# One level of Strassen-Winograd multiplication for a float32 input projection, in three token passes

## The chip, the cores and the metric

The kernel runs on one core of one Trainium2 chip. The metric is the device time of one execution in microseconds (us), taken as the median of several runs. All stages (short convolution, its output projection, keys and values, stick-breaking attention, decoding) are in one program, and each stage starts behind a barrier of all engines.

## What is computed

The change touches the first layer, a gated short convolution over 2048 prompt frames and 8 x 16 = 128 sample frames (2176 tokens, D = 1024):

```python
def _short_conv_mixer(xn, prev, w_in, conv_w, w_out):
    proj = xn @ w_in
    b_gate, c_gate, h, z = jnp.split(proj, 4, axis=-1)
    u = c_gate * h
    T = u.shape[1]
    up = jnp.concatenate([prev.astype(u.dtype), u], axis=1)
    conv = conv_w[0] * up[:, 0:T]
    for i in range(1, CONV_WIDTH):
        conv = conv + conv_w[i] * up[:, i:i + T]
    y = jax.nn.silu(z) * b_gate * conv
    return y @ w_out, up[:, T:]
```

Here `xn` is the RMS-normed input, `w_in` is 1024 x 4096, and the convolution is 3 taps wide. A layer adds the normed result to x.

## The kernel before

A float32 product is made of three fp32r products: every operand is split into a high part (a rounded copy) and a low part (the rest), and `project` (L349) issues high x high, high x low and low x high for each 128 rows of the contraction, eight times over K = 1024.

**Norming.** `phase_norm_in` (L112) takes the 17 tiles of 128 tokens. Per tile SP loads 512 KB; ACT squares and sums it and takes the root (L185, L188); DVE inverts (L209) and scales (L212); PE transposes it with 8 products by the identity (L248); ACT copies the result out of PSUM as the high part `a_xh` (L195) and DVE subtracts for the low part `a_xl` (L221). From the fifth tile on PE puts parts of the first strip's projection between the transposes (`project_group`, L231), so that it works while later tiles are normed. POOL splits the weights: two multiplications by the norm's gain and a subtraction of 128x1024 elements per strip (L285, L287, L289 in `split_weights`).

**Projection.** `phase_conv` (L408) then goes over 8 channel blocks c, and for each over the four matrices in the order c gate, h, z, b. Such a pair is called a strip here: 1024 x 128 weights against all 2176 tokens, in five groups of 512, 512, 384, 384, 384 tokens (`GROUPS`, L27), each in a PSUM bank of its own: 5 x 24 = 120 matmuls, 32 strips. PE waits at L487 for the group's bank to be read out, and at L485 for the split weights, of which there are two sets (names w_ and c_). ACT reads the c gate (L502) and z through SiLU (L506); DVE makes u = c * h (L537), the taps (L551 to L561), and the two gates (L566, L571); SP stores y for each block (L443). POOL runs one strip ahead (`weight_stream`, L308).

**Border to the output projection.** `Border` (L365) holds what the next stage, `phase_out` (L611), needs first: the first y tile, and the 8 row blocks of `a_w_out`, of which four are copied high (L399) and two low (L404) before the barrier. PE's first matmul of `phase_out` is at L762.

Of the kernel before, what the change touches and what calls it, by code (L numbers as in the profile page):

```python
# [111 lines left out]
def phase_norm_in(nc, x_prompt, x_sample, ident, ident_r, ident_in, epsb, xh, xl, consts, order, gain_in, room, pg):  # L112

    with ExitStack() as ctx:
        sb, pb, sem, sem2 = make_tools(nc, ctx)
        S = 4
        x_in = sb("n_x", [P, S, D])
        xs_at = (nc.sbuf_base + 31) // 32 * 32  # L120
        xs = sb("n_xs", [P, S, D])
        xs_bits = nc.alloc_sbuf_tensor_at("n_xs_bits", [P, S, D], F32R, offset=xs_at)
        junk = sb("n_junk", [P, D])
        ss = sb("n_ss", [P, S])
        std = sb("n_std", [P, S])
        rstd = sb("n_rstd", [P, S])
        ps = pb("n_ps", [P, 2, KT // 2, P])
        x_loaded = sem2("n_x_loaded", S)
        squared, std_ready, rstd_ready = sem2("n_squared", S), sem2("n_std", S), sem2("n_rstd", S)
        xs_ready, turned, hi_done, lo_done = sem2("n_xs_ready", S), sem2("n_turned"), sem2("n_hi"), sem2("n_lo")  # L130
        eps_set, ident_loaded, consts_loaded = sem("n_eps_set"), sem("n_ident_loaded"), sem("n_consts_loaded")
        ident_set = sem("n_ident_set")
        raw_loaded, gain_loaded, next_loaded = sem2("n_raw_loaded"), sem("n_gain_loaded"), sem("n_next_loaded")
        hi_ready, scaled, split = sem("n_w_hi"), sem("n_w_scaled"), sem("n_w_split")
        projected, passed, warm = sem("n_projected"), sem("n_passed"), sem("n_warm")
        HK = KT // 2
        raw, _, _, (gain, _) = room
        block = ctx.enter_context(nc.Block())

        @block.sync  # L140
        def _(sp):
            def load(j, s):
                sp.wait_ge(xs_ready[s], j)
                if is_sample(j, s, S):
                    src = x_sample
                else:
                    src = x_prompt[bass.ds((S * j + s) * P, P), :]
                sp.dma_start(x_in[:, s, :], src).then_inc(x_loaded[s], 16)

            for t in range(S):  # L150
                load(0, t)
                if t == 0:
                    sp.dma_start(ident[:, :], ident_in).then_inc(ident_loaded, 16)
            for m in range(2):
                sp.dma_start(raw[:, m, :, :], order[m][0](0)).then_inc(raw_loaded[m], 16)
            with sp.Fori(1, NT // S) as j:
                for s in range(S):
                    load(j, s)
            load(NT // S, 0)
            for dst, src in consts:  # L160
                sp.dma_start(dst, src, allow_slow_non_contiguous=True).then_inc(consts_loaded, 16)
            sp.wait_ge(consts_loaded, 16 * len(consts))

        @block.gpsimd
        def _(pool):
            load_gains(pool, [gain], [gain_in], gain_loaded)
            pool.wait_ge(gain_loaded, 16)
            for s in range(2):
                pool.wait_ge(raw_loaded[s], 16)
                split_weights(pool, room, s, order[s][1], hi_ready, scaled, split, s)  # L170
                pool.wait_ge(split, s + 1)
                apart(pool, passed)
                pool.dma_start(raw[:, s, :, :], order[2 + s][0](0)).then_inc(next_loaded, 16)
            pool.wait_ge(next_loaded, 32)

        @block.scalar
        def _(act):
            act.wait_ge(eps_set, 1)
            act.activation(std[:, 0:1], epsb[:, :], ACT.Sqrt).then_inc(warm, 1)
            act.wait_ge(warm, 1)  # L180

            def sums(j, s):
                act.wait_ge(x_loaded[s], 16 * (j + 1))
                act.wait_ge(rstd_ready[s], j)
                act.activation(junk[:, :], x_in[:, s, :], ACT.Square,  # L185
                               accum_out=ss[:, s:s + 1]).then_inc(squared[s], 1)
                act.wait_ge(squared[s], j + 1)
                act.activation(std[:, s:s + 1], ss[:, s:s + 1], ACT.Sqrt, scale=1.0 / D,  # L188
                               bias=epsb[:, :]).then_inc(std_ready[s], 1)

            def high(j, s):
                t = S * j + s
                for h in range(2):
                    act.wait_ge(turned[h], t + 1 + S * h)
                    act.activation(xh[:, h * HK:(h + 1) * HK, bass.ds(t * P, P)], ps[:, h, :, :],  # L195
                                   ACT.Copy).then_inc(hi_done[h], 1)

            token_tiles(act, sums, high, slots=S)
            act.activation(std[:, S - 1:S], epsb[:, :], ACT.Silu).then_inc(warm, 1)

        @block.vector
        def _(dve):
            dve.memset(epsb[:, :], EPS).then_inc(eps_set, 1)
            dve.wait_ge(ident_loaded, 16)
            dve.tensor_copy(ident_r[:, :], ident[:, :]).then_inc(ident_set, 1)

            def scale(j, s):
                dve.wait_ge(std_ready[s], j + 1)
                dve.reciprocal(rstd[:, s:s + 1], std[:, s:s + 1]).then_inc(rstd_ready[s], 1)  # L209
                dve.wait_ge(rstd_ready[s], j + 1)  # L210
                dve.wait_ge(turned[1], S * j + s + 1)
                dve.tensor_scalar(xs[:, s, :], x_in[:, s, :], rstd[:, s:s + 1], None,  # L212
                                  ALU.mult).then_inc(xs_ready[s], 1)

            def low(j, s):
                t = S * j + s
                at = bass.ds(t * P, P)
                for h in range(2):
                    half = slice(h * HK, (h + 1) * HK)
                    dve.wait_ge(hi_done[h], t + 1)  # L220
                    dve.tensor_tensor(xl[:, half, at], ps[:, h, :, :], xh[:, half, at].bitcast(F32),  # L221
                                      ALU.subtract).then_inc(lo_done[h], 1)

            token_tiles(dve, scale, low, slots=S)

        @block.tensor
        def _(pe):
            pe.sem_inc(turned[1], S)
            pe.wait_ge(ident_set, 1)

            def project_group(g, kt0, kt1):  # L231
                a, n = GROUPS[g]
                if kt0 == 0:
                    pe.wait_ge(split, 1)
                    for h in range(2):
                        pe.wait_ge(lo_done[h], (a + n) // P)
                mm = project(pe, pg[g][:, 0:n], room[1][0], room[2][0], xh, xl, a, n, kt0, kt1)
                if kt1 == KT:
                    mm.then_inc(projected, 1)

            for t in range(NT):
                j, s = divmod(t, S)
                pe.wait_ge(xs_ready[s], j + 1)
                for h in range(2):
                    wait_past(pe, lo_done[h], t)
                    for i in range(HK):
                        kt = h * HK + i
                        mm = pe.transpose(ps[:, h, i, :].bitcast(F32R), xs_bits[:, s, kt * P:(kt + 1) * P],  # L248
                                          ident_r[:, :])
                    mm.then_inc(turned[h], 1)  # L250
                for g in range(NG - 1):
                    t0, n = GROUPS[g + 1][0] // P, GROUPS[g + 1][1] // P
                    if t0 <= t < t0 + n:
                        project_group(g, (t - t0) * KT // n, (t - t0 + 1) * KT // n)
            project_group(NG - 1, 0, KT)
            pe.wait_ge(projected, NG)
# [12 lines left out]
def whole_room(sb, tag, room):  # L269

    raw, wh, wl, gains = room
    return raw, wh + [sb(tag + "wh1", [P, KT, P], F32R)], wl + [sb(tag + "wl1", [P, KT, P], F32R)], gains
# [2420 lines left out]
```

## Time and profile before

| | before |
|---|---|
| median of 3 runs | 2816.25 us (2815.89 to 2818.65) |
| the profiled execution | 2820.25 us, of which the span from first to last instruction 2818.7 us |
| granted TensorE clock, mean | 0.993 |
| PE busy | 2755.2 us (98%) |
| DVE, ACT, POOL busy | 1645.2, 1315.5, 1156.5 us |
| DMA | 433.33 MB, 154 GB/s on average |

The page cuts the span into 40 slices of 70 us; the convolution lies in the first 11 of them. PE reads 9 (90% or more) in each but the first, while DVE, ACT and POOL read 0 to 4 in most of them after the first two. A busy PE is not a PE at its peak: what a matmul costs is read from the distance between the starts of neighbours in the timeline, since its own duration includes its way through the array.

### The profile page before, as it was taken

The page shows a single profiled execution, that of the slowest core. Times are in us where ns is not written, and L with a number is a line of the kernel's source. Part 1 is how long each engine was busy: PE and PEld are TensorE (multiplying, and loading weights), DVE is VectorE, ACT ScalarE, POOL GpSimd, SP SyncE. Part 2 cuts the span into 40 slices and gives each one's busy share as a digit, 9 for nine tenths or more (in the row PEclk, how much of TensorE's full clock was granted, in tenths as well). Part 3 has the DMA queues.
Part 4 walks back from the last instruction along what each step waited for, and adds up shares of the span by engine and source line. Part 5 has one row for each costly group of instructions (what it writes and reads, how often), then busy time and mean ns, then how long its engine had stood idle before and what let it go on. Part 6 is the DMA issues. An engine that isn't in the chain of part 4 may idle for free. (4 is left out here: it accounts for less than half of the span.)

```text
span 2818.7 us, 42045 instructions
## 1 busy us (share of the span) xinstructions
PE 2755.2 (98%) x14856; PEld 2409.4 (85%) x14856; DVE 1645.2 (58%) x2152; ACT 1315.5 (47%) x2733; POOL 1156.5 (41%) x1023
## 2 busy tenths in 40 slices
PE   7999999999999999999989999999999999979998
PEld 6999999999978888889978888888888888868886
DVE  5321232123244450102249999999999999998775
ACT  6000000000034441111148888888888888875543
POOL 3333333233210020002356877777777768651110
PEclk9999999999999999999999999999999999999999
DMA  5101110111064444424578676777777866766873
GB/s 160 38 24 38 38 38 22 38 38 38 9 202 131 136 152 153 174 102 157 166 219 269 197 245 198 237 215 217 223 222 207 251 203 207 224 184 203 239 229 107
DMA packets 280359, 433.33 MB, mean 154 GB/s; under 512 B 52578, under 2 KB 218594, under 8 KB 274180
## 3 DMA queue, kind: packets, MB, share of 16 engines
q1 hardware_dynamic: 269156, 391.41, 45.4%
q0 software_dynamic: 11040, 39.86, 4.7%
q8 instruction: 89, 1.46, 0.2%
q14 instruction: 74, 0.61, 0.1%
HBM read 307.40 MB, written 123.81 MB: 153 GB/s over the span
## 5 line engine op out<-in xcount | busy, mean ns | idle before, releaser
L1994 POOL TENSOR_TENSOR a_a<-a_a,a_prod 128x512 f32<-128x512 f32 (+3 forms) x640 | 661.1, 1051 | 270.3 <-DVE a_prod L1945 196.0
L1945 DVE TENSOR_TENSOR_SCAN a_prod<-a_keep,a_prod,a_restart 128x513 f32<-128x513 f32 x384 | 478.0, 1269 | 7.5 <-ACT a_keep L1889 5.7
L1888 ACT ACTIVATE a_a<-a_pz 128x512 f32<-128x512 f32 (+3 forms) x640 | 357.4, 559 | 69.4 <-PE a_pz L1815 44.4
L1955 DVE TENSOR_TENSOR a_atl<-a_pt,a_ath 128x512 fp32r<-128x512 f32 (+3 forms) x640 | 363.0, 599 | 33.0 <-ACT a_ath L1898 29.9
L1889 ACT ACTIVATE a_keep<-a_pz 128x512 f32<-128x512 f32 (+3 forms) x640 | 361.4, 565 | 0.0
L1898 ACT ACTIVATE a_ath<-a_pt 128x512 fp32r<-128x512 f32 (+3 forms) x640 | 333.0, 558 | 57.8 <-PE a_po L1829 34.2
L1838 PEld LDWEIGHTS a_pt<-ident_r,a_bits 128*128 128x128 f32 x2176 | 231.4, 141 | 51.1 <-DVE a_atl L1955 7.4
L285 POOL TENSOR_TENSOR w_wh<-w_raw,w_gain 128x1024 fp32r<-128x1024 f32 x22 | 41.7, 1897 | 534.2 <-PE v_pg L355 278.9
L1814 PE MATMUL a_pz<-a_kh,a_q 128*128 128x512 f32 (+3 forms) x640 | 246.9, 389 | 8.7 <-ACT a_keep L1889 6.2
L1827 PE MATMUL a_po<-a_ath,a_v 128*128 128x512 f32 (+3 forms) x640 | 250.8, 396 | 2.7 <-POOL a_v L2005 1.9
L1838 PE MATMUL a_pt<-ident_r,a_bits 128*128 128x128 f32 x2176 | 244.2, 241 | 6.4 <-DVE a_atl L1955 4.2
L1815 PE MATMUL a_pz<-a_kl,a_q 128*128 128x512 f32 (+3 forms) x640 | 233.7, 367 | 0.0
L353 PE MATMUL c_pg<-a_xh,w_wh 128*128 128x384 f32 (+1 forms) x640 | 231.3, 361 | 0.0
L353 PE MATMUL c_pg<-a_xh,c_wh 128*128 128x384 f32 (+1 forms) x640 | 230.7, 360 | 0.3 <-ACT c_cgate L502 0.3
L354 PE MATMUL c_pg<-a_xl,w_wh 128*128 128x384 f32 (+1 forms) x640 | 230.5, 360 | 0.0
L354 PE MATMUL c_pg<-a_xl,c_wh 128*128 128x384 f32 (+1 forms) x640 | 230.5, 360 | 0.0
L355 PE MATMUL c_pg<-a_xh,c_wl 128*128 128x384 f32 (+1 forms) x640 | 230.4, 360 | 0.0
L1829 PE MATMUL a_po<-a_atl,a_v 128*128 128x512 f32 (+3 forms) x640 | 229.7, 368 | 0.0
L355 PE MATMUL c_pg<-a_xh,w_wl 128*128 128x384 f32 (+1 forms) x640 | 228.9, 358 | 0.0
L537 DVE TENSOR_TENSOR c_u<-c_pg,c_cgate 128x512 f32<-128x512 f32 (+2 forms) x40 | 23.4, 585 | 317.9 <-PE c_pg L355 317.9
L1939 DVE TENSOR_TENSOR_SCAN a_prod<-a_keep,a_restart 128x128 f32<-128x128 f32 (+3 forms) x256 | 197.1, 805 | 9.0 <-ACT a_keep L1889 8.2
L506 ACT ACTIVATE c_sz<-c_pg 128x384 f32<-128x384 f32 (+1 forms) x40 | 21.4, 536 | 355.8 <-PE c_pg L355 355.8
(234 smaller groups left out, 6128.0 us busy)
## 6 DMA issues: line engine op xcount, KB each, us to landing
a_x<-x_d SPq DMA_DIRECT2D x84, 896.0 KB, 6.7
a_x<-x_d SPq DMA_DIRECT2D x56, 832.0 KB, 5.9
a_kh<-kh_t SPq DMA_DIRECT2D x32, 512.0 KB, 6.9
a_kl<-kl_t SPq DMA_DIRECT2D x32, 512.0 KB, 8.8
w_raw<-in_a_w_in POOLq DMA_DIRECT2D x30, 512.0 KB, 4.8
x<-f_xn POOLq DMA_DIRECT2D x17, 512.0 KB, 5.9
g_y_in<-sz_t SPq DMA_DIRECT2D x17, 512.0 KB, 7.9
g_x<-x SPq DMA_DIRECT2D x17, 512.0 KB, 3.6
```

The costliest lines, as they stand in the source:

```text
L353: pe.matmul(out, w_h[:, kt, :], x_h[:, kt, r], start=(kt == 0), stop=False)
L354: pe.matmul(out, w_h[:, kt, :], x_l[:, kt, r], start=False, stop=False)
L355: mm = pe.matmul(out, w_l[:, kt, :], x_h[:, kt, r], start=False, stop=(kt == KT - 1))
L1814: pe.matmul(o, lhs, kh2[hh][:, p0:p0 + w], start=True, stop=False)
L1827: pe.matmul(o, v2[hh][:, kb, :, :], ath[:, b % AS, c0:], start=first, stop=False, skip_group_check=True)
L1838: mm = pe.transpose(pt[:, turn_slot(pr, hh, b), q * P:(q + 1) * P].bitcast(F32R), a_bits[:, unit_slot(hh, u), q, j * P:(j + 1) * P], ident ...
L1888: act.activation(a[:, s, q, 0:w], pz[:, n % ZS, 0:w], ACT.Sigmoid, scale=SCALE)
L1889: act.activation(keep[:, n % KS, 0:w], pz[:, n % ZS, 0:w], ACT.Sigmoid, scale=-SCALE).then_inc(z_used, 1)
L1898: act.activation(ath[:, b % AS, c0:], pt[:, turn_slot(pr, hh, b), c0:], ACT.Copy).then_inc(at_hi, 1)
L1945: dve.tensor_tensor_scan(prod[:, s, 0:w + 1][:, ::-1], keep[:, n % KS, 0:w + 1][:, ::-1], restart[:, 0:1].broadcast_to([P, w + 1]), prod[: ...
L1955: dve.tensor_tensor(atl[:, b % AS, c0:], pt[:, turn_slot(pr, hh, b), c0:], ath[:, b % AS, c0:].bitcast(F32), ALU.subtract).then_inc(at_spl ...
L1994: pool.tensor_tensor(part, part, prod[:, n % PS, after:after + w], ALU.mult).then_inc(weighted, 1)
```

## The change

The projection's operands are cut in two along both dimensions: K into two halves of 512, a pair of weight matrices (c gate and h, or z and b) as the two output halves, and the tokens of a pass into two halves. The four output quarters then come from seven products instead of eight, by Winograd's form: the weights enter as A11, A12, A22 and four sums S1 to S4, the tokens as B11, B21, B22 and four differences T1 to T4. The outputs are put together by five additions out of PSUM.

- The tokens go in three passes, of 2 x 320, 2 x 384 and 2 x 384. A pass has 16 strips (8 channel blocks x 2 pairs of matrices), a strip 7 products, a product 4 x 3 = 12 matmuls of 320 or 384 columns: 84 a strip, 4032 in all (before: 3840 of 512 or 384).
- The weights are loaded anew in each pass, 1 MB a strip, now by SP's queue. POOL makes S1 to S4 (`sums`, four operations of 128x512). ACT makes every high part (seven of 128x512 a strip), DVE every low part. The gain is multiplied into the tokens (`stage`), no longer into the weights.
- Only the first 5 tiles are normed ahead; the other 12 are normed in odd strips of passes 0 and 1, all of the scaling by ACT.
- At the first strip of a pass each of the seven token operands (512 rows x 320 or 384 tokens, 4 x w elements a partition) is split anew by ACT and DVE, just before its product needs it, and POOL makes the differences (DVE two of them in pass 0).
- u = c * h, the gates and the last product move from DVE to POOL, out of SBUF; the first tap moves to ACT.
- SP's queue now carries the weight loads, the x tiles and the y stores in one written order.
- In `Border` five blocks of `a_w_out` are split high and low before the barrier.

PE's order in a strip n is A11, S1, A22 of strip n - 1, S2, A12, S4, S3. Its core, and what each product waits for:

```diff
+PASSES = [(0, 320), (640, 384), (1408, 384)]
...
+                if n >= 2 and i == A11_B11:
+                    pe.wait_ge(c11_read, n - 1)
...
+                elif i == A12_B21:
+                    pe.wait_ge(p1_read, n + 1)
+                elif i == S4_B22:
+                    pe.wait_ge(v_read, n + 1)
+                elif i == S3_T3:
+                    pe.wait_ge(u2_read, n + 1)
+                elif i == A22_T4:
+                    pe.wait_ge(c22_read, n + 1)
+                if first_of_pass(n):
+                    pe.wait_ge(x_lo[i], p + 1)
+                pe.wait_ge(w_lo[i], n + 1)
+                o = bank(n, b, w)
+                for k in range(NH):
+                    x_h, x_l = room.xh[i][:, k, 0:w], room.xl[i][:, k, 0:w]
+                    pe.matmul(o, room.wh[i][:, k, :], x_h, start=fresh and k == 0, stop=False, skip_group_check=True)
+                    pe.matmul(o, room.wh[i][:, k, :], x_l, start=False, stop=False, skip_group_check=True)
+                    mm = pe.matmul(o, room.wl[i][:, k, :], x_h, start=False, stop=k == NH - 1, skip_group_check=True)
...
+            for t in range(FIRST_TILES):
+                turn(t)
+            for n in range(NSTRIP):
...
+                product(n, A11_B11)
+                product(n, S1_T1)
+                if n:
+                    product(n - 1, A22_T4)
+                product(n, S2_T2)
+                product(n, A12_B21)
+                product(n, S4_B22)
+                product(n, S3_T3)
```

DVE's strip, and SP's and POOL's:

```diff
+                if n:
+                    c22(n - 1)
+                    low(n, S3_T3)
+                low(n + 1, A11_B11)
+                dve.wait_ge(done[S1_T1], n + 1)
...
+                add(room.v[:, 0:w], n, BANK_B, room.p1[:, n % 2, 0:w], v_read)
+                low(n + 1, S1_T1)
+                if n:
+                    c21(n - 1)
+                low(n, A22_T4)
...
+                add(room.u2[:, 0:w], n, BANK_C, room.p1[:, n % 2, 0:w], u2_read)
+                low(n + 1, S2_T2)
+                if n % 2:
+                    taps(n)
+                low(n + 1, A12_B21)
...
+                if n >= 0 and n + 2 < NSTRIP:
+                    sp.wait_ge(w_lo[A22_T4], n + 1)
+                    sp.wait_ge(summed, 4 * (n + 1))
+                    apart(sp, passed_sp)
+                    load_raw(n + 2, 1)
+                if n >= 2 and n % 2 == 0:
+                    store(n - 1)
...
+                if n and n % 2:
+                    set_u(n - 1, 1)
+                if n + 1 < NSTRIP:
+                    sums(n + 1)
+                if n and n % 2 == 0:
+                    gate(n - 1, 0)
+                    gate(n - 1, 1)
+                    finish(n - 1, 1)
```

How the instructions stand. First DVE in one channel block of the projection before (u, the edge copies, the taps; `c_t` is the convolved tile):

```order
L537 TENSOR_TENSOR c_u<-c_pg,c_cgate 128x512 x2
L537 TENSOR_TENSOR c_u<-c_pg,c_cgate 128x384 x2
L537 TENSOR_TENSOR c_u<-c_pg,c_cgate 128x256
L539 TENSOR_TENSOR c_us<-c_pg,c_cgate 128x8x16
L547 COPY c_edge<-c_u 128x2
L548 COPY c_edge<-c_us 128x16
L551 TENSOR_SCALAR c_t<-c_u,c_cw 128x2048
```

And DVE now in strip 15, the last of pass 0, from the middle of which the operands of pass 1 are split (`c_wl` and `c_xl` are low parts of weights and tokens, `c_pc` is PSUM, `c_v`, `c_sums`, `c_u_118` take its sums):

```order
L699 TENSOR_TENSOR c_wl_84<-c_raw_91,c_wh_77 128x512
L692 TENSOR_TENSOR c_xl_70<-c_stage,c_xh_63 128x1536
L706 TENSOR_TENSOR c_v<-c_pc,c_p_117 128x320
L699 TENSOR_TENSOR c_wl_85<-c_s_107,c_wh_78 128x512
L692 TENSOR_TENSOR c_xl_71<-c_t_94,c_xh_64 128x1536
L706 TENSOR_TENSOR c_sums<-c_pc,c_p_117 128x320
L699 TENSOR_TENSOR c_wl_90<-c_raw_92,c_wh_83 128x512
L706 TENSOR_TENSOR c_u_118<-c_pc,c_p_117 128x320
L699 TENSOR_TENSOR c_wl_86<-c_s_108,c_wh_79 128x512
L692 TENSOR_TENSOR c_xl_72<-c_stage,c_xh_65 128x1536
L727 SCALAR_TENSOR_TENSOR c_t<-c_u,c_taps,c_t 128x640 x2
```

Before, DVE touched PSUM or the convolution's tiles only; now the reads of PSUM that PE waits for stand in one queue with the splits of weights and tokens.

POOL before, one pair of strips (`w_raw` is the loaded weight tile):

```order
L285 TENSOR_TENSOR w_wh<-w_raw,w_gain 128x1024
L287 TENSOR_TENSOR w_raw<-w_raw,w_gain 128x1024
L289 TENSOR_TENSOR w_wl<-w_raw,w_wh 128x1024
L326 DMA w_raw<-in_a_w_in 128x8x128
L285 TENSOR_TENSOR c_wh<-w_raw,w_gain 128x1024
```

And POOL now at the same strip 15 (`c_s` are the weight sums, `c_stage` and `c_t_94` hold the tokens and T1):

```order
L865 TENSOR_TENSOR c_u<-c_sums,c_cg 128x320
L817 TENSOR_TENSOR c_s_107<-c_raw_91 128x512
L820 TENSOR_TENSOR c_s_108<-c_s_107,c_raw_91 128x512
L822 TENSOR_TENSOR c_s_109<-c_raw_91 128x512
L825 TENSOR_TENSOR c_s_110<-c_raw_91,c_s_108 128x512
L839 TENSOR_TENSOR c_stage<-c_stage,c_t_94 128x4x384
L865 TENSOR_TENSOR c_u<-c_sums,c_cg 128x320
L845 TENSOR_TENSOR c_stage<-c_stage 128x4x384
```

The weight DMAs are gone from POOL's queue; in it are now the sums, the products of the gating, and between them at a pass's end the token differences.

## Rows read from the trace of the kernel before

**Rows 1.** Windows: us, then each engine's busy time, PE clock, DMA share
```profile
22.20:61.20 39.00, 36.93 (x218) 31.04 (x218) 27.79 (x49) 29.77 (x61) 7.06 (x4) 1.00 0.50 148
62.13:794.70 732.57, 732.57 (x3728) 667.31 (x3728) 191.26 (x212) 48.03 (x86) 221.02 (x118) 1.00 0.12 38
```

**Rows 2.** Waits from 62 to 797 us: total, times, longest
```profile
DVE c_u L537 <- PE c_pg L355: 317.9, 40, 27.0
...
POOL c_wh L285 <- PE c_pg L355: 237.8, 15, 17.4
...
PE c_pg L353 <- ACT c_cgate L502: 0.3, 1, 0.3
```

**Rows 3.** Groups by shape, two of PE's twelve for the projection
```profile
L354 PE MATMUL c_pg<-a_xl,w_wh 128*128 128x384 f32 x384 | 129.0, 336 | 0.0
...
L353 PE MATMUL c_pg<-a_xh,c_wh 128*128 128x512 f32 x256 | 101.6, 397 | 0.3 <-ACT c_cgate L502 0.3
```

**Rows 4.** Timeline of PE: start, duration; 24 matmuls apart, then 20 apart
```profile
786.65 0.34 PE L355 MATMUL c_pg<-a_xh,c_wl 128*128 128x384 f32 x1
...
790.81 0.34 PE L355 MATMUL c_pg<-a_xh,c_wl 128*128 128x384 f32 x1
...
2697.28 0.29 PE L2323 MATMUL s_pzo<-s_kth,s_pad_h 128*128 128x272 f32 x1
...
2699.79 0.29 PE L2325 MATMUL s_pzo<-s_kth,s_pad_l 128*128 128x272 f32 x1
```

**Rows 5.** Timeline of the start and of the norming
```profile
4.64 1.06 ACT L185 ACTIVATE n_junk<-n_x 128x1024 f32<-128x1024 f32 x1 [2.15 <-issue]
...
8.48 1.06 ACT L185 ACTIVATE n_junk<-n_x 128x1024 f32<-128x1024 f32 x1 [2.37 <-DMA n_x<-in_x_prompt]
...
22.23 0.76 PE L353 MATMUL c_pg<-a_xh,w_wh 128*128 128x512 f32 x1
...
38.06 0.80 PE L248 MATMUL n_ps<-ident_r,n_xs_bits 128*128 128x128 f32 x8
38.70 0.47 PE L353 MATMUL c_pg<-a_xh,w_wh 128*128 128x512 f32 x1
```

**Rows 6.** Timeline of PE across the barrier before the output projection
```profile
794.45 0.34 PE L355 MATMUL c_pg<-a_xh,c_wl 128*128 128x384 f32 x1
797.31 0.47 PE L762 MATMUL f_ph<-b_xh,f_yh 128*128 128x512 f32 x1 [2.52 <-PEq L102]
...
798.68 0.63 PE L764 MATMUL f_ph<-b_xh,f_yl 128*128 128x512 f32 x1
799.11 0.63 PE L762 MATMUL f_ph<-b_xh,f_yh 128*128 128x512 f32 x1
```

**Rows 7.** Timeline of POOL, then of DVE, where both work from SBUF
```profile
280.03 2.41 POOL L289 TENSOR_TENSOR c_wl<-w_raw,c_wh 128x1024 fp32r<-128x1024 f32 x1
...
278.12 1.92 DVE L552 TENSOR_SCALAR c_t<-c_us,c_cw 128x128 f32<-128x128 f32 x1
280.07 4.52 DVE L554 SCALAR_TENSOR_TENSOR c_t<-c_u,c_cw,c_t 128x2048 f32<-128x2048 f32 x1
...
284.88 2.35 DVE L559 SCALAR_TENSOR_TENSOR c_t<-c_u,c_cw,c_t 128x2048 f32<-128x2048 f32 x1
```

**Rows 8.** Groups and timeline rows that price the new operations
```profile
L2018 POOL TENSOR_TENSOR w_raw<-w_raw,w_gain 128x512 f32<-128x512 f32 x26 | 27.1, 1042 | 23.6 <-POOLq L102 21.6 <-PE a_pq L1858 1.9
...
797.16 6.91 DVE L404 TENSOR_TENSOR b_xh<-b_x,b_xh 128x1024 fp32r<-128x1024 f32 x6 [1.77 <-PEq L102]
...
L571 DVE TENSOR_TENSOR c_sz<-c_pg,c_t 128x384 f32<-128x384 f32 x24 | 13.4, 558 | 79.0 <-PE c_pg L355 79.0
...
797.14 3.90 ACT L399 ACTIVATE b_xh<-b_x 128x1024 fp32r<-128x1024 f32 x4 [4.07 <-PEq L102]
...
L502 ACT ACTIVATE c_cgate<-c_pg 128x384 f32<-128x384 f32 x24 | 11.6, 494 | 76.3 <-PE c_pg L355 76.3
...
w_raw<-in_a_w_in POOLq DMA_DIRECT2D x30, 512.0 KB, 4.8
```

More of the change, by code:

```diff
@@ L109, in make_tools @@
     return sb, pb, sem, sem2
[L112 to L256, printed above, removed]
@@ L405, in low_weights @@
                               self.wh(kt, slice(0, D)).bitcast(F32), ALU.subtract).then_inc(self.w_lo, 1)
[L408 removed]
+NH = KT // 2
+PASSES = [(0, 320), (640, 384), (1408, 384)]
+PW_MAX = 384
+NPASS = len(PASSES)
+STRIPS = [(p, c, m) for p in range(NPASS) for c in range(KT) for m in range(2)]
+NSTRIP, PER_PASS = len(STRIPS), 2 * KT
+FIRST_TILES = 2 * PASSES[0][1] // P
+A11_B11, S1_T1, S2_T2, A12_B21, S4_B22, S3_T3, A22_T4 = range(7)
@@ new lines, in _ @@
+            sp.wait_ge(y_stored[0], 16 * KT)
+            for i in (A11_B11, A12_B21, A22_T4):
+                sp.wait_ge(w_lo[i], LAST)
+            sp.wait_ge(summed, 4 * LAST)
+            apart(sp, passed_sp)
+            border.load_tile(sp)
+            for i in (A11_B11, S1_T1):
+                sp.wait_ge(done[i], NSTRIP)
+            apart(sp, passed_sp)
+            border.load_weights(sp, range(AHEAD, KT))
+            sp.wait_ge(e_rows, 2)
+            apart(sp, passed_sp)
+            sp.dma_start(conv_p, room.edge_rows[0:2, :]).then_inc(e_stored, 16)
@@ new lines, in turn @@
+            def turn(t):
+                pe.wait_ge(scaled, t + 1)
+                out = turned_at(t)
+                wait_past(pe, staged, 2 * (t - 1 if t < FIRST_TILES else t))
+                if t == FIRST_TILES:
+                    pe.wait_ge(st_ready, 1)
+                for kt in range(KT):
+                    mm = pe.transpose(out[:, kt, :].bitcast(F32R), room.norm_bits[room.scaled(t)][:, kt * P:(kt + 1) * P],
+                                      ident_r[:, :])
+                mm.then_inc(turned, 1)
@@ new lines, in _ @@
+            act.wait_ge(eps_set, 1)
+            act.activation(room.std[:, 0:1], epsb[:, :], ACT.Sqrt).then_inc(warm, 1)
+            act.wait_ge(warm, 1)
+            for t in range(FIRST_TILES):
+                sums_of(t)
+                if t:
+                    scale(t - 1)
+                if t == 3:
+                    high_w(0, A11_B11)
+                elif t == 4:
+                    high_x(0, A11_B11)
+            scale(FIRST_TILES - 1)
+            high_w(0, S1_T1)
+            high_x(0, S1_T1)
@@ L576, in begin_next, with inverse, stage @@
-            def begin_next(g):
-                if g == 1:
+            def inverse(t):
+                dve.wait_ge(std_ready, t + 1)
+                dve.reciprocal(room.rstd[:, t:t + 1], room.std[:, t:t + 1]).then_inc(rstd_ready, 1)
+            def stage(t):
+                p = next(p for p in range(NPASS) if t * P < sum(tokens_of(p)[::2]))
+                at = t * P - PASSES[p][0]
+                dve.wait_ge(turned, t + 1)
+                if t == 0:
+                    dve.wait_ge(gain_loaded, 16)
+                for h in range(2):
+                    half = slice(NH * h, NH * (h + 1))
+                    dve.tensor_tensor(room.stage[:, half, at:at + P], turned_at(t)[:, half, :],
+                                      gain[:, half].unsqueeze(2).broadcast_to([P, NH, P]), ALU.mult).then_inc(staged, 1)
@@ new lines, in add, with c22, c21 @@
+            def add(out, n, b, other, read):
+                w = width(n)
+                dve.tensor_tensor(out, bank(n, b, w), other, ALU.add).then_inc(read, 1)
+            def c22(n):
+                w = width(n)
+                dve.wait_ge(done[S3_T3], n + 1)
+                wait_past(dve, u_set if n % 2 else y_done, 2 * pair(n) + (1 if n % 2 else -1))
+                dve.wait_ge(v_read, n + 1)
+                add(room.sums[:, 1, 0:w], n, BANK_C, room.v[:, 0:w], c22_read)
+            def c21(n):
+                w = width(n)
+                dve.wait_ge(done[A22_T4], n + 1)
+                wait_past(dve, u_set if n % 2 else y_done, 2 * (pair(n) + n % 2))
+                add(room.sums[:, 0, 0:w], n, BANK_C, room.p1[:, n % 2, 0:w], c21_read)
@@ new lines, in _ @@
+            dve.memset(epsb[:, :], EPS).then_inc(eps_set, 1)
+            dve.wait_ge(ident_loaded, 16)
+            dve.tensor_copy(ident_r[:, :], ident[:, :]).then_inc(ident_set, 1)
+            dve.memset(room.u[:, 0:2], 0.0).then_inc(cleared, 1)
+            inverse(0)
+            for t in range(FIRST_TILES):
+                if t + 1 < FIRST_TILES:
+                    inverse(t + 1)
+                if t == 3:
+                    low(0, A11_B11)
+                stage(t)
+            dve.wait_ge(staged, 2 * FIRST_TILES)
@@ L580, in begin_next @@
                                       ALU.subtract).then_inc(border.y_lo, 1)
-                elif 2 <= g < 2 + LOW_AHEAD:
-                    border.low_weights(dve, range(g - 2, g - 1))
-            with dve.Fori(0, KT - 1) as c:
-                conv_and_gate(c)
-            conv_and_gate(KT - 1)
+                k = n - PER_PASS * (NPASS - 1) - 7
+                if 0 <= k < AHEAD:
+                    border.low_weights(dve, range(k, k + 1))
+            c22(LAST)
+            c21(LAST)
+        @block.gpsimd
```

666 lines of the change are left out of this document (470 added, 196 removed).

## The prediction

> **What bounds the kernel now.** I read the 40 slices first (PE at 9 in all the convolution's slices but the first), then the windows [rows 1]: from 62.13 to 794.70 us PE has no gap at all, at full granted clock, while DVE, ACT and POOL work 191, 48 and 221 us of 733. Then the waits [rows 2]: in that stretch the other engines wait for PE for hundreds of us, and PE waits 0.3 us for anybody. The stage is bound by the number of columns that PE streams, so fewer columns pay in full, for as long as the other engines keep up. Only the start (first projection matmul at 22.23 us, norming until 61.2) and the barrier (794.45 to 797.31) hold something else [rows 5, 6].
>
> **PE's steady part.** The distance of neighbours is the price of a matmul. 24 matmuls of 384 columns are 4.16 us apart, 0.1733 each; 20 of 272 columns are 2.51 us apart, 0.1255 each [rows 4]. A line through both gives 0.146 for 320 columns, a width that no row shows. 31 strips take 732.57 us [rows 1], 23.6 each; without 72 x 0.1733 that leaves 11.1 us for 48 matmuls of 512, 0.232 each. The whole stage has 12 x 128 = 1536 of 512 columns and 6 x 384 = 2304 of 384 [rows 3]: 356 + 399 = 755 us. After it: 1344 of 320 and 2688 of 384, 196 + 466 = 662 us. PE's work falls by 93 us, an eighth.
>
> The Trainium skill (TensorE: Matmul & The Clock Gate, Back-to-back issue gap) gives columns / 2.4 + 2.5 ns for an isolated warm matmul, that is 0.136 us at 320 and 0.1625 at 384. By it the stage would go from about 706 to 619 us, a gain of 87 instead of 93; the trace's 0.1733 at 384 speaks against it, and the measured distances stand.
>
> **What a strip asks of the others.** DVE copies of 1024 elements a partition out of SBUF cost 6.91 / 6 = 1.15 us, so 512 about 0.60, 1536 about 1.7, 1280 about 1.4; a DVE operation on 384 PSUM columns 0.56 (320: 0.49); the taps at 2.35 us for 2048 elements are 0.88 for 768 and 0.74 for 640; ACT's copy is 3.90 / 4 = 0.98 for 1024, so 0.55 to 0.6 for 512, and 0.49 for 384 of PSUM; POOL takes 1.04 for 512, so I take 0.78 for 384, 0.65 for 320, 3.1 for 1536 [rows 7, 8]. A strip of pass 0 lasts 84 x 0.146 = 12.3 us on PE, one of the others 84 x 0.1733 = 14.6. In it DVE has 7 low parts (4.2), 5 additions out of PSUM (2.45 or 2.8), on average one tap operation (0.74 or 0.88): 7.4 or 7.9 us, and 0.7 more where tiles are staged. POOL has 4 sums (4.2) and 3 products (1.95 or 2.3): 6.1 or 6.5. ACT has 7 high parts and under 2 us more: 6, and with a tile's norming 5 more in two strips. A weight load lands in 4.8 us [rows 8] and is issued about 6 us before POOL wants it. Each engine alone has time to spare.
>
> DVE and POOL are not alone, though. While POOL works from 280.03 to 282.44, a DVE operation of 2048 elements takes 4.52 us where its twin takes 2.35: it waited POOL out; so did one on 128 elements, 1.92 us [rows 7]. They took turns by whole operations. Counting only what works out of SBUF on both, a strip of pass 0 needs 4.2 + 0.7 + 6.1 = 11.0 of 12.3 us, one of the others 11.6 of 14.6. It fits, tightly in pass 0. The reads that PE waits for have room in the written order: v two to three products after its source is done, u2 two, c22 two (1.75 us a product in pass 0). Followed through an odd strip of pass 0 (taps and staging both in it) DVE comes some 3 us late to c22 and has 3.5. I take **5 us** of waits for all six such strips; low end nothing, high end the serial case below.
>
> The Trainium skill (SBUF — State Buffer, Who interferes with whom) states this as an exclusive lock: a DVE instruction with two SBUF inputs and a POOL one that reads SBUF block each other for the whole instruction, while DVE with one SBUF input goes free. The rows agree. It is the rule that speaks against this change, which moves work to POOL's SBUF side and gives DVE seven new two-input operations a strip; what it costs is the rival of the serial case.
>
> **The start.** Before, PE projects from 22.23 us on, between transposes. Now ACT does square, sum, root and scale for each of five tiles, about 2.6 us each, from the tile at 8.48 on [rows 5], and some weights and tokens: 21.7. Transposing 1.3 and staging 1.4 lead to 24.4. Then stand on DVE: two differences (2.9), five products' splits at 0.6 + 1.4 (10), then v, three more weight splits, the seventh operand's tokens and u2 (0.5 + 1.8 + 1.4 + 0.5 = 4.2) before S3 of strip 0 may run, at 41.5, and end 1.8 later, at 43.3. On the same SBUF side POOL has two differences (2.6 each) and four sums (4.2) to do in that time, 9.4 us; if DVE waits all of them out, S3 ends at 52.7. That is the end of strip 0's six products, 72 matmuls. The ends are 43.3 and 52.7; I take **52.7**, since the first strip's chain has no backlog of products to hide behind.
>
> **The pass borders.** At strips 15 and 31 DVE gets five token splits of 1.7 us before c22, and POOL four differences of 3.1 around them. Without blocking, DVE reaches c22 of strip 15 19.7 us after the strip's start, PE wants it at 16.1; at the second border the lack is 2: together 6, the low end. If port use were gapless from strip 14 on, the operations of both until u2 of strip 16 sum to 51 us against 33 available, and 52 against 37: lags of 18 and 15, and 3 for the clock, 36 us, the high end. I take 12 + 9, and 3 for the clock: after the 2.9 us without matmuls at the barrier, PE ran on for 1.4 us and then took 0.43 instead of 0.23 us a matmul, the lower of its two levels (1.2 GHz), for some seven matmuls [rows 6]. Sum **24**, above the middle, since each split here meets a POOL operation three times as long as usual.
>
> **The rest.** 12 tiles are transposed within the strips, as before: 0.64 to 0.87 us of PE for eight [rows 5], 9.0. State and edge transposes 1.5. Last matmul to the first of the output projection: 2.86 before [rows 6]; behind it now stand c21, a POOL product, the last y store and the barrier: 3.5. Five split blocks of `a_w_out` instead of two and four are worth nothing, since PE's first tile there ran at its distance but for the slow clock. Code without loops costs nothing: PE ran gapless through the unrolled last block (to 794.70) already. DMA moves 32 MB more, under 50 GB/s more where 38 flowed.
>
> **Sum**, to the first matmul at L762: 52.7 + 1272 x 0.146 (185.7) + 2688 x 0.1733 (465.8) + 9.0 + 1.5 + 24 + 5 + 3.5 = 747.2 us, against 797.3: 50.1 us less. The profiled execution's 2820.25 becomes 2770; the median of the runs lies 4.0 lower, at 2816.25, so I forecast 2816.25 - 50 = **2766 us**. Of 93 us saved on PE about half comes back: 14 at the start, 24 at the borders, 5 in strips.
>
> **The rivals.**
> - *Serial DVE and POOL* (0.22). In each strip DVE's 7.4 to 8.6 and POOL's 6.1 to 6.5 add up without overlap, because DVE always finds POOL in an operation. Then a strip of pass 0 takes 14.2, not 12.3 (16 x 1.9 = 30), and one of pass 1 15.1, not 14.6 (9); pass 2 still fits. 39 in place of 5: 2800. For it: both wait in order, and rows 7. Against it: DVE's PSUM additions, 2.5 us a strip, run beside POOL.
> - *Clean* (0.12). Waiting at the start and the borders overlaps with PE's backlog: 6 less at the start, 14 at the borders, 3 in strips: 2743.
> - *Narrow matmuls save nothing* (0.05). 320 columns cost what 384 do, by some floor in the weight load: 1272 x 0.027 = 35 more, 2801. Against it: 0.1255 at 272 columns.
> - *Slower* (0.08): a recurring lag that drops the clock. If, once in each pair of strips, DVE comes so late (taps, staging and POOL's blocking in the odd strip) that PE stands 2.5 us, each time followed by slow matmuls as behind the barrier (1.4 us), that is 24 x 3.9 = 94 us: 2860. It decides from about 2.1 us a pair of strips on. Against it: the margin above, and full granted clock in all stretches between barriers.
> - *Forecast as it stands* (0.53), by itself 2750 to 2786.
>
> The range 2742 to 2803 takes in all but the slower case and the tails. A measurement of this kernel tells 0.2% (5.6 us) from no change. Faster 0.91, within 0.2% 0.01, slower 0.08.
>
> **What would show it.** PE at 0.146 and 0.173 us between neighbours; first L762 matmul near 747 us; PE's idle time in three clumps (until 53, after strips 15 and 31) of about 12 us each at the borders, released by DVE's PSUM additions; DVE's 512-element low parts showing means well above 0.69 us, POOL's sums above 1.04. It would be wrong if idle time is spread over all strips (serial or slower case), if the granted clock falls in the passes, or if 320 columns stand 0.17 apart.

## The result and the profile after

The forecast was wrong in sign. The changed kernel takes **2835.14 us** (median of 4 runs, 2833.93 to 2840.28), the kernel before, run beside it, 2817.45 us (2815.89 to 2821.12): a ratio of 1.0064, 95% interval 1.0047 to 1.0082. So it is slower by 0.5 to 0.8%, outside the range that was given (2742 to 2803). The profiled execution has a span of 2832.2 us (2818.7 before) and a mean granted clock of 0.980 (0.993 before).

The first matmul of the output projection (line 1086 now) starts at 812.31 us; before it started at 797.31 [rows 6], forecast was 747.2. From there to the end the kernels agree: 2832.2 - 812.31 = 2019.9 us, against 2818.7 - 797.31 = 2021.4. The miss, 65.1 us, lies whole in what stands ahead of that matmul.

The windows of the profile after, cut at the pass borders, answer to [rows 1] (columns as there, with DMA rate last):

```profile
54.70:244.50 189.80, 178.65 (x1227) 176.68 (x1227) 144.07 (x200) 108.21 (x184) 131.21 (x98) 1.00 0.35 101
244.50:295.40 50.90, 33.88 (x171) 32.42 (x170) 43.23 (x33) 20.59 (x29) 40.46 (x19) 0.80 0.17 48
295.40:522.30 226.90, 216.34 (x1226) 214.43 (x1225) 155.15 (x202) 110.87 (x190) 132.42 (x99) 0.97 0.31 91
522.30:570.80 48.50, 33.58 (x170) 32.81 (x169) 42.35 (x32) 20.98 (x30) 38.12 (x18) 0.82 0.18 52
570.80:812.00 241.20, 228.00 (x1281) 225.39 (x1280) 168.76 (x218) 94.62 (x192) 149.00 (x112) 0.98 0.30 92
```

The 732.57 us without a gap are gone. PE stands idle in every window, most at the two borders (strips 15 and 16, 31 and 32), where the clock falls to 0.8 as well. No engine is full anywhere; DVE comes nearest, at the first border (43.23 of 50.90 us, POOL 40.46). The waits of PE from 62 to 812 us (total, times, longest) name what was late; [rows 2] had 0.3 us there:

```profile
PE c_pc L474 <- DVE c_sums L706: 32.8, 7, 12.0
PE c_pt L486 <- ACT c_norm L532: 21.1, 12, 1.8
PE c_pc L474 <- DVE c_u L706: 7.4, 3, 3.9
PE c_pc L474 <- DVE c_v L706: 2.0, 1, 2.0
```

Three places hold nearly all of it. **The tiles.** Twelve times, at the start of the odd strips from 3 to 13 and from 19 to 29, PE waits 1.76 us for a normed tile before it can transpose it (timeline of PE, then of ACT, at strip 5):

```profile
109.59 0.87 PE L486 MATMUL c_pt<-ident_r,c_norm_bits 128*128 128x128 f32 x8 [1.76 <-ACT c_norm L532]
```
```profile
106.11 0.64 ACT L554 ACTIVATE c_wh<-c_s 128x512 fp32r<-128x512 f32 x1 [0.81 <-PE c_pc L476]
107.87 0.63 ACT L554 ACTIVATE c_wh<-c_s 128x512 fp32r<-128x512 f32 x1 [1.12 <-PE c_pc L476]
108.41 1.13 ACT L532 ACTIVATE c_norm<-c_norm,c_rstd 128x1024 f32<-128x1024 f32 x1
```

ACT idles 1.12 us for a product of PE, copies the weights' high part for S3, and scales the tile only then. What it idles for is the last product of the strip, since the high parts of S3 overwrite those that this product reads. PE has nothing left to do but the transposes that wait for the scaling. Behind the wait of strips 19, 21, 25 and 27 some ten matmuls of 384 columns stand 0.32 us apart instead of 0.1733 (granted clock 0.56 from 329 to 331 us in strip 19, 1.00 before the wait): these are the slow matmuls spoken of below, at the lower of the clock's two levels for most of that stretch.

**The output projection's weights.** From strip 39 on a block of `a_w_out` is split at the end of each DVE strip, ahead of `c22`, which PE waits for before A22 of the strip behind. DVE, and PE at strip 42:

```profile
704.92 0.69 DVE L699 TENSOR_TENSOR c_wl<-c_s,c_wh 128x512 fp32r<-128x512 f32 x1 [3.58 <-ACT c_wh L554]
...
711.52 1.22 DVE L214 TENSOR_TENSOR b_xh<-f_raw,b_xh 128x1024 fp32r<-128x1024 f32 x1
712.66 0.55 DVE L706 TENSOR_TENSOR c_sums<-c_pc,c_v 128x384 f32<-128x384 f32 x1
```
```profile
713.26 0.69 PE L474 MATMUL c_pc<-c_xh,c_wh 128*128 128x384 f32 x1 [3.93 <-DVE c_sums L706]
```

The operation of 1.22 us alone does not explain 3.93 us. The delay begins one strip earlier, where the same operation first waits for ACT's high part of the block (DVE, then POOL, then ACT):

```profile
692.23 1.23 DVE L214 TENSOR_TENSOR b_xh<-f_raw,b_xh 128x1024 fp32r<-128x1024 f32 x1 [2.36 <-ACT b_xh L209]
693.38 0.55 DVE L706 TENSOR_TENSOR c_sums<-c_pc,c_v 128x384 f32<-128x384 f32 x1
```
```profile
694.01 0.84 POOL L861 TENSOR_TENSOR c_us<-c_sums,c_cg 128x128 f32<-128x128 f32 x1 [4.76 <-DVE c_sums L706]
```
```profile
703.04 0.20 ACT L592 ACTIVATE c_edge<-c_u 128x2 f32<-128x2 f32 x1 [4.54 <-POOL c_u L865]
```

So c22 of strip 40 comes late. PE does not stand there, but POOL waits 4.76 us for it before it makes its products and sums, ACT waits 4.54 us for POOL, DVE 3.58 us for ACT, and only then is c22 of strip 41 late for PE.

**The pass borders.** DVE's, ACT's and POOL's timelines at strip 15 (L706 `c_sums<-c_pc,c_v` is c22):

```profile
268.31 0.69 DVE L699 TENSOR_TENSOR c_wl<-c_s,c_wh 128x512 fp32r<-128x512 f32 x1 [5.24 <-ACT c_wh L554]
...
275.75 3.74 DVE L699 TENSOR_TENSOR c_wl<-c_s,c_wh 128x512 fp32r<-128x512 f32 x1
279.41 2.81 DVE L692 TENSOR_TENSOR c_xl<-c_stage,c_xh 128x1536 fp32r<-128x1536 f32 x1
282.15 0.48 DVE L706 TENSOR_TENSOR c_sums<-c_pc,c_v 128x320 f32<-128x320 f32 x1
```
```profile
266.84 0.20 ACT L590 ACTIVATE c_carry<-c_u 128x2 f32<-128x2 f32 x1 [7.88 <-POOL c_u L865]
```
```profile
262.09 3.89 POOL L839 TENSOR_TENSOR c_stage<-c_stage,c_t 128x1536 f32<-128x1536 f32 x1
265.93 0.87 POOL L865 TENSOR_TENSOR c_u<-c_sums,c_cg 128x320 f32<-128x320 f32 x1
275.51 3.43 POOL L845 TENSOR_TENSOR c_stage<-c_stage 128x1536 f32<-128x1536 f32 x1 [8.71 <-DVE c_xl L692]
```

POOL makes `c_u` behind a difference of 3.89 us, ACT waits 7.88 us for it in `keep_and_tap`, DVE 5.24 us for ACT. Then DVE works without a gap, stands under POOL's next difference (3.74 us for an operation that takes 0.69 alone, while POOL works from 275.51 to 278.94), and PE gets c22 after 10.56 us of idleness.

### The profile page after: what moved, and what is told of

Read it like the earlier page. It is cut to its first block and busy times, and to the rows that moved or that the text cites. A ratio compares the mean times of both kernels' runs of the same rounds, so it can differ in the third digit from the quotient of the medians.

```text
span 2832.2 us, 44315 instructions
## 1 busy us (share of the span) xinstructions
PE 2690.6 (95%) x15048; PEld 2407.0 (85%) x15048; DVE 1998.5 (71%) x2590; ACT 1606.5 (57%) x3224; POOL 1435.6 (51%) x1251
## 5 line engine op out<-in xcount | busy, mean ns | idle before, releaser
L474 PE MATMUL c_pc<-c_xh,c_wh 128*128 128x384 f32 (+1 forms) x1344 | 453.3, 337 | 58.3 <-DVE c_sums L706 32.8
L476 PE MATMUL c_pc<-c_xh,c_wl 128*128 128x384 f32 (+1 forms) x1344 | 449.2, 334 | 0.0
L475 PE MATMUL c_pc<-c_xl,c_wh 128*128 128x384 f32 (+1 forms) x1344 | 449.2, 334 | 0.0
L2212 ACT ACTIVATE a_a<-a_pz 128x512 f32<-128x512 f32 (+3 forms) x640 | 357.4, 559 | 70.2 <-PE a_pz L2139 48.5
L474 PEld LDWEIGHTS c_pc<-c_xh,c_wh 128*128 128x128 f32 x1344 | 261.5, 195 | 63.9 <-DVE c_sums L706 35.9
L475 PEld LDWEIGHTS c_pc<-c_xl,c_wh 128*128 128x128 f32 x1344 | 261.3, 194 | 0.0
L476 PEld LDWEIGHTS c_pc<-c_xh,c_wl 128*128 128x128 f32 x1344 | 261.0, 194 | 0.0
L699 DVE TENSOR_TENSOR c_wl<-c_s,c_wh 128x512 fp32r<-128x512 f32 x192 | 199.2, 1037 | 69.9 <-ACT c_wh L554 65.1
L554 ACT ACTIVATE c_wh<-c_s 128x512 fp32r<-128x512 f32 x192 | 120.5, 629 | 176.3 <-PE c_pc L476 138.3
L699 DVE TENSOR_TENSOR c_wl<-c_raw,c_wh 128x512 fp32r<-128x512 f32 x144 | 152.7, 1060 | 94.0 <-ACT c_wh L554 92.3
```

The source lines that it names most:

```text
L474: pe.matmul(o, room.wh[i][:, k, :], x_h, start=fresh and k == 0, stop=False, skip_group_check=True)
L475: pe.matmul(o, room.wh[i][:, k, :], x_l, start=False, stop=False, skip_group_check=True)
L476: mm = pe.matmul(o, room.wl[i][:, k, :], x_h, start=False, stop=k == NH - 1, skip_group_check=True)
L699: dve.tensor_tensor(room.wl[i][:, :, :], room.weights(n, i), room.wh[i][:, :, :].bitcast(F32), ALU.subtract).then_inc(w_lo[i], 1)
L2212: act.activation(a[:, s, q, 0:w], pz[:, n % ZS, 0:w], ACT.Sigmoid, scale=SCALE)
```

## The experiments

Each undoes or moves one part of the changed kernel. The yardstick is the start of the first matmul of the output projection (812.31 us in the changed kernel; called F below) and the length of single strips on PE. F has some noise of its own: over the variants, none of which touches strip 0, that strip takes 31.4 to 33.7 us (33.4 in the changed kernel; why it varies is not shown), and slow matmuls behind the waits vary by up to 3 us.

**The tile waits.** Theory: an order of waits, as above. Two edits, one on each side of the wait.

```diff
-                if n >= 2 and n - 2 in norm_of:
-                    turn(norm_of[n - 2])
...
                 product(n, A11_B11)
+                if n >= 2 and n - 2 in norm_of:
+                    turn(norm_of[n - 2])
                 product(n, S1_T1)
```

> PE's transposes of a normed tile are issued behind A11 of the strip instead of ahead of it. Theory 'written order': PE waits 1.76 us at each of 12 tiles only because ACT's scaling stands behind a weight copy that waits for the strip's last product; behind A11 (2.1 us) the scaling is done. 21 us of waits go, and some 6 us of slow clock in strips 19 to 27 with them: 27 us less, first matmul of the output projection at about 785 us instead of 812.3. Theory 'throughput' (DVE and POOL are too slow on the shared SBUF side, the wait only shows it): the tile comes later to DVE's staging, waits come back at DVE's additions, 5 us less at most.

Measured: 2813.37 us, ratio to before 0.998 (0.997 to 0.999); F 788.64, 23.7 less. An odd strip of pass 0 with its tile takes 13.3 us instead of 12.4 + 2.6, one of pass 1 15.3, and the slow matmuls behind it are gone. In pass 1 (strips 17 to 29) all of the waits and slow matmuls go, 18.3 us. In pass 0 (strips 1 to 13) 6.4 of the 6 x 1.76 = 10.6 us of waits go: in strips 4, 6, 8 and 10 PE now waits 0.7 to 0.8 us for DVE's c22, where it had not waited before:

```profile
122.45 0.41 PE L474 MATMUL c_pc<-c_xh,c_wh 128*128 128x320 f32 x1 [0.72 <-DVE c_sums L706]
```

So the throughput theory holds for a part of pass 0: the tile's wait had covered a smaller one. The borders (strips 14 to 16 and 30 to 32) give 4.6 us back as well; strip 0 is 2.1 us shorter by its noise.

```diff
                 high(n + 1, S4_B22)
+                if n - 1 in norm_of:
+                    scale(norm_of[n - 1])
                 high(n + 1, S3_T3)
...
-                if n - 1 in norm_of:
-                    scale(norm_of[n - 1])
```

> Edit: ScalarE scales the normed tile one step earlier, ahead of the high parts of S3 (which wait for the last product of the strip), and TensorE's transposes stay where the change put them. Theory, TensorE waits 1.8 us twelve times because the scaling stands behind a wait for the strip's own end: the gap of 2.6 us at the start of strips 2, 4 and so on falls to 0.9 to 1.2 (the transposes alone), as it did when the transposes were moved; first matmul of the output projection at 788 to 796 against 812.3. Rival, ScalarE has no room for the scaling at any place: gap 2 us or more, or as much before S3 in the strip ahead.

Measured, in one run: 2816.26 us, F 790.9. The time between the strips falls from 2.63 to 1.09 us in pass 0 (0.22 of it still a wait) and 0.65 in pass 1 (the transposes alone); 0.6 us come back before A22 in strips 4, 6, 8 and 10, as above. The expectation counts the tiles by the strip that they follow. PE at strip 5, where 1.76 us stood:

```profile
106.17 0.88 PE L486 MATMUL c_pt<-ident_r,c_norm_bits 128*128 128x128 f32 x8 [0.22 <-ACT c_norm L532]
```

Either side of the wait gives nearly the same F (788.6 and 790.9), so ACT had the time, only not at that place in its order.

**The output projection's weights.** DVE's low parts of `a_w_out` go behind `low(n, A22_T4)` of the next strip:

```diff
                 low(n, A22_T4)
+                k = n - 1 - PER_PASS * (NPASS - 1) - 7
+                if 0 <= k < AHEAD:
+                    border.low_weights(dve, range(k, k + 1))
...
-                k = n - PER_PASS * (NPASS - 1) - 7
-                if 0 <= k < AHEAD:
-                    border.low_weights(dve, range(k, k + 1))
```

> The five low parts of a_w_out leave the place just ahead of the addition c22 in DVE's queue and go behind the low part of A22, one strip later. Same work for DVE. Theory 'written order': the waits before A22 in pass 2 (4.1, 4.1, 1.2 us in strips 42, 44, 40, and the slow clock behind them, 4 us) shrink to about 3 us in all: 10 us less. Theory 'throughput': DVE has the same work in the strip, the waits stay: within 3 us of no change.

Measured: 2821.64 us, ratio 1.0009 (1.0000 to 1.0019); F 796.86, 15.5 less. Strips 40, 42 and 44 take 14.8, 14.6 and 14.7 us instead of 15.9, 20.3 and 21.5, with the same work on each engine: 13.5 of the 15.5 us, and the rest is mostly strip 0. An operation of 1.22 us and DVE's wait for its input, ahead of c22, cost PE up to 6.9 us in a strip, slow matmuls included.

**The borders: what fills them.** Work is left out at the second border only; the first is the control.

```diff
+                    if p == 2:
+                        pool.sem_inc(t_set[0], 1)
+                        pool.wait_ge(t_set[0], p + 1)
+                        pool.sem_inc(t_set[1], 1)
+                        return
```

> Leaves out POOL's four differences of the tokens for the last pass (the counts go on), so pass 2 multiplies other numbers. If POOL's queue and its share of the SBUF side make the pass border long, strips 31 and 32, now 18.7 + 29.8 us against 12.3 + 14.6 of matmuls, lose most of their 21 us excess: 8 us or less is left. If DVE's own six to seven token splits do, 15 us or more is left.

```diff
+                if p == 2:
+                    act.sem_inc(x_hi[i], 1)
+                    return
                 act.activation(room.xh[i][:, :, 0:w], room.operand(p, i), ACT.Copy).then_inc(x_hi[i], 1)
```

DVE's low parts are left out in the same way, and so are POOL's `second_difference` and `third_difference`.

> Leaves out ACT's and DVE's splits of the seven token operands for the last pass (the counts go on), POOL's differences stay. If DVE's splits make the border long, the excess of strips 31 and 32 (21 us) falls to 3 us or less; if POOL's queue does, 10 us or more is left.

> Left out: of the last pass's tokens, both GpSimd's differences and the high and low parts (so the products of the last pass use old parts). Alone, each had cut strips 31 and 32 from 48.5 us to 41.0 and 38.8 (without waits they take 27.0, worked out from 12.4 and 14.6). Theory, the two kinds of token work bound the border together: without both, strips 31 and 32 take 27 to 29 us and TensorE's wait before A22(31) is under 1 us. Rival, the written order of waits bounds it whatever the work: strips 31 and 32 still take over 34 us, with 5 us or more before A22(31).

Strips 31 and 32 together, 48.51 us in the changed kernel (29.2 if nothing waited): 40.98 without POOL's differences, 38.80 without the splits, 29.18 without both. The expectations counted strip 31 as one of pass 0 (12.3 us of matmuls); it has 384 columns, so the excess was 19.3 us and not 21. The first two runs by themselves decided nothing (11.8 and 9.6 us of excess left, between the bounds that they had been given), as each left about 8 us of waiting before A22(31). Without both, the windows of strips 31, 32 and 33 are:

```profile
520.30:534.80 14.50, 14.50 (x85) 14.50 (x84) 10.15 (x12) 5.99 (x11) 10.05 (x7) 1.00 0.22 62
534.80:549.40 14.60, 14.60 (x86) 14.60 (x85) 11.00 (x15) 5.80 (x12) 10.22 (x8) 1.00 0.36 103
549.40:564.00 14.60, 14.60 (x86) 14.60 (x85) 9.61 (x12) 6.28 (x13) 10.10 (x8) 1.00 0.25 70
```

PE has no gap left, though every wait stands in the same order; the untouched first border still waits 11.79 us at A22(15). The token work makes the second border's loss; that the first border's has the same cause is inferred from its like pattern, not shown. The savings alone (7.5 and 9.7) come to 17.2 of 19.3 us, so each kind costs about its own share and 2 us come of both.

**The borders: does the order matter?** GpSimd's product first, then, apart, c22 first:

```diff
+                if n and n % 2:
+                    set_u(n - 1, 0)
                 if n % PER_PASS == PER_PASS - 1 and n < PER_PASS * (NPASS - 1):
                     second_difference(n // PER_PASS + 1)
-                if n and n % 2:
-                    set_u(n - 1, 0)
```

> Edit: in the last strip of a pass GpSimd makes the first half of the gated product (set_u of strips 14 and 30) before the second token difference, not behind it; nothing else is changed. Theory of written order: ScalarE's keep_and_tap(15) waits for that product, the high parts of S2 stand behind it and VectorE idles 5.3 us for them, so both borders shrink by 2 to 4 us each: time 2827 to 2832 us, first matmul of the output projection at 804 to 809 against 812.3. Rival, the token work itself fills the border whatever its order: within 1 us of the changed kernel at the first matmul of the output projection, since the difference that is moved back delays the high and low parts of S3 by as much.

```diff
                 if n:
-                    c22(n - 1)
+                    if not first_of_pass(n):
+                        c22(n - 1)
...
+                if n < LAST and first_of_pass(n + 1):
+                    c22(n)
                 low(n + 1, S4_B22)
```

> Edit: at the two pass borders VectorE adds c22 of the pass's last strip (which TensorE's A22 product waits for) ahead of the low parts of S4 of the next pass, not behind them. Theory of written order: A22(15) and A22(31) start as soon as c22 can be made, 3 to 6 us earlier; some comes back as a wait of S4(16) for its token split, so that 2 to 5 us a border are left: time 2825 to 2831 us, first matmul of the output projection at 802 to 808. Rival, work bounds the border: the wait moves whole from A22 to S4 of the same strip, within 1 us at the first matmul of the output projection.

Product first: 2832.53 us, ratio 1.0048 (1.0033 to 1.0064), F 805.07. ACT's and DVE's waits shrink (DVE's 5.24 to 1.82 us), and the borders by 2.3 and 0.9 us, 3.2 in all; the rest of the 7.2 at F are slow matmuls and strip 0, which this edit doesn't touch. c22 first: 2837.0 us, ratio 1.0068 (1.0052 to 1.0083), F 809.04; of the 3.3 us less at F 2.0 are strip 0, and the borders don't shrink. PE's timeline at the first border:

```profile
274.26 0.64 PE L474 MATMUL c_pc<-c_xh,c_wh 128*128 128x320 f32 x1 [5.46 <-DVE c_sums L706]
285.81 0.69 PE L474 MATMUL c_pc<-c_xh,c_wh 128*128 128x384 f32 x1 [3.62 <-DVE c_v L706]
```

The wait of 10.56 us is halved and comes back before S4(16) and S3(16); strips 15 and 16 take 52.7 us (50.9), 31 and 32 48.4 (48.5). That is the rival's answer: DVE has more to do than PE's backlog covers, and these two orders only choose the product at which PE stands. Other orders were not tried.

**Together.**

> Edit: the transposes of the normed tile one product later, and VectorE's low parts of the output projection's weights behind the low parts of the next strip's A22. If the two losses are separate, the savings add: 23.7 + 15.5 us less to the first matmul of the output projection, 773 us, and a time of 2798 to 2801 us, below the kernel before (2818.8) by 0.6 to 0.7 per cent. Rival, they share what they wait for (ScalarE and GpSimd late as a whole): at most 30 us in all, 782 us and 2805 us or more.

Tiles and weights: 2801.16 us (2798.43 to 2805.09), ratio 0.9935 (0.9919 to 0.9950); F 776.89, 35.4 less, where 39.2 would be the plain sum. Of the 3.8 us between them 2.1 are the shorter strip 0, which is in both single runs and can count only once; from strip 1 on it is 33.5 of 35.2, and the slow matmuls of strips 42 and 44 account for 1.2 of what is left.

> Edit: both edits of the run before it, and at the pass borders GpSimd's product ahead of the second difference and VectorE's c22 ahead of the low parts of S4. Theory of written order: the borders lose a further 10 to 18 us in all: first matmul of the output projection at 755 to 764 us, time 2782 to 2791 us. Rival, the borders are bound by the token work itself: at most 3 us below the run with two edits. In either case faster than the kernel before.

Both, with product and c22 first: 2804.13 us, ratio 0.9940 (0.9926 to 0.9953), F 781.09 (strip 0 again longer, by 2.3): no gain on the two, as the rival had it.

> Edit: transposes one product later, low parts of the output projection's weights one strip later, and at the two pass borders GpSimd's product ahead of the second difference; the c22 edit is left out, since it only moved the wait to S4. If each saves beside the others what it saved alone: first matmul of the output projection at 770 to 774 (776.9 with the first two), time 2795 to 2799 us, ratio to before 0.992 to 0.994. If the third saves nothing once the transposes are moved: within 1.5 us of 2801.

Both, with the product first alone: **2800.20 us** (2794.33 to 2802.57), ratio 0.9925 (0.9912 to 0.9939). The borders lose 2.3 us against the two edits, strip 0 takes 2.0 more; the medians differ by less than either kernel's runs. Both versions beat the kernel before by 0.6 to 0.8%, and the change by 1.2%.

## Why the prediction was wrong

The sum had 747.2 us to F, and F came at 812.31. From the starts of the strips on PE; what a strip takes over its matmuls at 0.1463 and 0.1733 us goes to the step that it belongs to:

| step | forecast | measured |
|---|---|---|
| start, six products of strip 0 | 52.7 | 54.7 |
| 3960 matmuls | 651.5 | 652.0 |
| 12 tiles, with the slow matmuls behind them | 9.0 | 38.8 |
| pass borders | 24 | 43.7 |
| split of `a_w_out` (strips 40, 42, 44) | 0 | 14.0 |
| other strips, state and edge | 6.5 | 5.1 |
| barrier | 3.5 | 4.0 |

- **Columns: right.** In the timeline of PE, 24 matmuls of 320 columns are 3.51 us apart, 0.1463 each (0.146), and strips without a gap take 12.4 and 14.6 us (12.3, 14.6). So the "narrow" rival is out; the 0.136 us that follows for 320 columns from the formula for an isolated matmul in the Trainium skill (TensorE: Matmul & The Clock Gate, Back-to-back issue gap) is not what these pairs of load and matmul took. PE's busy time in the program fell from 2755.2 to 2690.6 us, and the stage got longer all the same.

```profile
90.08 0.31 PE L474 MATMUL c_pc<-c_xh,c_wh 128*128 128x320 f32 x1
...
93.59 0.31 PE L474 MATMUL c_pc<-c_xh,c_wh 128*128 128x320 f32 x1
...
812.31 0.77 PE L1086 MATMUL f_ph<-b_xh,f_yh 128*128 128x512 f32 x1 [3.84 <-PEq L102]
```

- **The start: right,** 2.0 us over the upper end that was chosen. PE's longest wait there is 8.0 us for u2, the addition that the prediction named ahead of S3.
- **"12 tiles are transposed within the strips, as before: ... 9.0": the step that failed most,** 29.8 of 65 us. The transposes were priced, 0.87 us for eight, and not the arrival of what they read. ACT had 6 of 12.3 us to do, with 5 more for a tile in two strips, and from that I took it to be on time. But its order has the scaling behind a wait for the strip's own end. Each tile cost 2.63 us, and 1.5 more in strips 19, 21, 25 and 27, where slow matmuls followed.
- **"Five split blocks ... are worth nothing": failed, 14.0 us.** I looked at what PE did behind the barrier and not at what stands behind the new operation in DVE's queue, which is c22, nor at what it waits for, which is the last thing in ACT's strip.
- **The borders: mechanism right, size off** by 19.7 us. The high end of 36 had been worked out without ACT's wait for POOL, and POOL's prices were low: 1.04 us for 512 elements came from an operation with a broadcast row; the sums here take 1.34 to 1.50 us on average (pass 1) and 1.26 at the least, the differences 3.43 to 3.95 instead of 3.1. How much of that is the operand and how much DVE's work beside it is not shown.
- **DVE and POOL in the steady strips: right, in part by luck.** They slow each other (low parts 1.00 to 1.04 us on average, 0.69 alone), yet strips without a tile run at PE's pace. The "serial" rival is out: most excess has an address. The 5 us forecast for DVE late at c22 in pass 0 do not show here, because the tile's wait gives DVE the time; with the transposes moved they come out, 0.7 to 0.8 us in each of strips 4, 6, 8 and 10. One reading of [rows 7] went too far: the operation of 1.92 us has a single SBUF tensor as input, so it is no case of two inputs, and that one input "goes free" is not borne out by it; it ended at 280.04, just behind the operation of POOL that ran beside it (to 279.96; its line is below), and so in all eight blocks. DVE's additions out of PSUM, with one SBUF input, did run beside POOL: 0.55 us on average in pass 1, as priced.
- **The "slower" rival** had the right shape, a short wait that recurs and slow matmuls after some of them, and another culprit: DVE at c22, at 94 us. It was ACT at the tile, at 30.

Groups by shape of the profile after, POOL and DVE in pass 1:

```profile
L817 POOL TENSOR_TENSOR c_s<-c_raw 128x512 f32<-128x512 f32 x14 | 21.0, 1502 | 30.9 <-issue 30.9
L822 POOL TENSOR_TENSOR c_s<-c_raw 128x512 f32<-128x512 f32 x14 | 18.8, 1345 | 13.8 <-DVE c_wl L699 13.8
...
L831 POOL TENSOR_TENSOR c_t<-c_stage 128x1536 f32<-128x1536 f32 x1 | 4.0, 3952 | 0.0
```
```profile
L699 DVE TENSOR_TENSOR c_wl<-c_raw,c_wh 128x512 fp32r<-128x512 f32 x43 | 44.8, 1042 | 44.7 <-ACT c_wh L554 43.8
```

And POOL in the timeline of the kernel before, beside the rows of [rows 7]:

```profile
276.98 2.98 POOL L287 TENSOR_TENSOR w_raw<-w_raw,w_gain 128x1024 f32<-128x1024 f32 x1
```

What stays open: of the first border's loss the runs show no split into its parts.

## What to carry to other kernels

A balance of busy time per strip tells whether an engine can keep up, not whether a result is there when it is wanted. For each thing that the bounding engine waits for, walk the producer's queue backwards to the last wait in it: if that wait is for the bounding engine's own latest work, it is a gap each time round, however idle the producer. And before an order is blamed, leave the work out: the tiles and `a_w_out` were order, and moving one operation paid 13.5 of 14.0 us at `a_w_out` and all of the tile waits in pass 1, but only 6.4 of 10.6 us in pass 0, where the next late operation showed; the second border was work, and at both borders moving one operation mostly moved the wait.

## What was not expected of the hardware

The same gap does not always bring the lower clock. In pass 0 of the changed kernel, none of the six gaps of 2.63 us between matmuls of 320 columns was followed by slow matmuls; over the six variants that keep these gaps one of 36 was (c2_nosplit, strip 3: 1.5 us lost, granted clock 0.57 from 81 to 85 us). In pass 1, with 384 columns, four of six were, each time 1.5 us lost, and in the variants three or four of six in other strips. Gaps of 1.2 us in pass 2 brought none, those of 4.1 us always 1.5 to 2.9, those of 10.7 to 13.8 brought 1.5 to 3.0. What decides between equal gaps is not shown.
